# Values and output gates of the matrix memory as seven products of quarters, with row sums shared by GpSimd and VectorE

## The chip, the cores and the metric

One Trainium2 chip, of which the kernel uses one core. The metric is device time in microseconds: the median of the runs of the kernel on that core. Lower is better. The engines named are TensorE (PE; PEld are its weight loads), VectorE (DVE), ScalarE (ACT), GpSimd (POOL) and SyncE (SP), which issues the loads.

## What is computed

Two transformer-like blocks over 2048 tokens of width 1024, in float32. The first block norms and modulates its input, projects it with one wide matrix, and sends the parts to neighbourhood attention on a grid and to a matrix memory (mLSTM) that runs both ways over the sequence. The part that matters here, cut from the reference:

```python
proj = h @ w_in + b_in                      # h: 2048 x 1024
(..., ml_q, ml_k, ml_v, ml_o, ml_z, i_f, f_f, i_b, f_b) = jnp.split(proj, split_idx, axis=-1)
qk = jax.nn.silu(centred_short_conv(jnp.concatenate([ml_q, ml_k], axis=-1), conv_w, conv_b))  # 5 taps
h_fwd = mlstm_chunkwise(mq, mk, mv, i_f, f_f)
h_bwd = flip(mlstm_chunkwise(flip(mq), flip(mk), flip(mv), flip(i_b), flip(f_b)))
hm = (h_fwd + h_bwd) * jax.nn.sigmoid(ml_o)
hm = (hm - mu) * lax.rsqrt(var + EPS) * ml_norm_w
ml_out = hm * jax.nn.silu(ml_z)
```

There are 4 heads of 128 channels. `ml_v` (values) and `ml_o` (output gates) of a head are each the 2048 x 1024 rows times a 1024 x 128 slice of weights, plus a bias.

## The kernel before, in words

The function `mlstm` (L313) runs after `modulate_and_norm`, which leaves the normed rows turned in `hT` (128 partitions, 8 pieces of 128 channels, 2048 tokens). It is one block in which every engine has its own program, in program order, and the engines meet at semaphores. The order of the work is written out by hand. The heads are taken one after the other (head 0 to head 3 below; x in the code).

For each head there are three projections by channels (keys, queries, gate z): `project` (L578), 12 blocks of 8 matmuls 128x512 at L600 into `bank[0]` and `bank[1]`, evicted by ScalarE (`evict`, L745 and L750). Those of head x + 1 are spread over the state and chunk loops of head x, two matmuls at a time. Then, with nothing else on TensorE, comes the stage that the change rewrites: `project_turned` (L604 to L615), 8 blocks (4 of values, 4 of output gates), each 4 tiles of tokens x 8 matmuls 128x128 at L614, with tokens on the partitions of the result. VectorE adds the bias while it copies a block out (`put`, L854 to L866) into `v1` or `og`.

What the other engines do beside that stage: VectorE convolves the queries (`convolve`, L838: one tensor_scalar at L848 and four taps, scalar_tensor_tensor of 2048 columns, at L851) and scales the keys (`scale_keys`, L872), in the order of `values` (L925). For head 0 the five steps of the keys' convolution come first. ScalarE applies silu to the keys (L810) as soon as their convolution is done, then to the queries (L812) when theirs is, and only then enters the state loop.

The state loop has 15 steps: TensorE turns two chunks of keys (`turn`, L628), ScalarE weighs them (`weigh`, L757), TensorE multiplies them with the values (`product`, L637 to L645) and, behind that in its queue, runs two matmuls of the next head's projections; VectorE adds the result to the carried state (`carry`, L880). At its second step ScalarE applies the sigmoid to all of `og` (L819). In the chunk loop follow scores, decays, products with the state (L651, L656, L662) and sums (`add_up`, L903; `divide`, L917); GpSimd masks the rows of decays (`mask`, L542), adds both directions and multiplies by the gate (`combine`, L548 and L550). Then VectorE takes moments, norms (sixteen tensor_scalars, L1000), convolves the next head's keys, and scales the turned outputs into `mix` (`put_head`, L923), for which TensorE turns them (`turn_out`, L672) between projections. The order there is four times `turn_out`, two matmuls of projection, and then the next head's stage.

SyncE loads each weight slice (`load`, L451, issued at L459) when the product that used its room is done.

Of the kernel before, what the change touches and what calls it, by code (L numbers as in the profile page):

```python
# [8 lines left out]
ALU = mybir.AluOpType  # L9
# [3 lines left out]
P = 128  # L13
T = 2048
D = 1024
KC = D // P
# [296 lines left out]
def mlstm(nc, t, hT, mix, c_act, w_first, w_first_in, roll):  # L313
# [6 lines left out]
    with ExitStack() as ctx:  # L320
# [82 lines left out]
        out_dve = sem("l_out_dve")  # L403
# [30 lines left out]
        NB = 4 * NW  # L434
        NA = 4 * V_

# [7 lines left out]
        def evicted(n):  # L444

            return (out_act, n + 1, NA) if n < NA else (out_dve, n - NA + 1, NB - NA)

        with nc.Block() as block:
            @block.sync
            def _(sp):  # L450
                def load(x, s):  # L451
                    if x > LAST:
                        return
                    if s == O_ and x == LAST:
                        sp.wait_ge(proj, NB * x + 4)
                    elif x > 0:
                        sp.wait_ge(proj, NB * (x - 1) + 4 * s + 4)
# [10 lines left out]
                def fetch_bias(x):  # L468
                    if x > LAST:
                        return  # L470
                    need(sp, out_dve, (NB - NA) * x)
# [30 lines left out]
                for x in range(ML_HEADS):  # L502
# [16 lines left out]
                    if x == LAST - 1:  # L519
                        ada_v = t["w_ada"].rearrange("a (k p) n -> p (a k) n", p=P)  # L520
                        sp.wait_ge(proj, NB * ML_HEADS)
# [5 lines left out]
                sp.wait_ge(proj, NB * ML_HEADS)  # L527
# [9 lines left out]
            def _(pool):  # L537
                def mask(x, b):
                    pool.wait_ge(rb_in[b % 2], 16 * (2 * x + b // 2 + 1))
                    view = rb[:, b % 2].rearrange("p d (c l) -> p d c l", l=P)  # L540
                    for dr in range(2):
                        nc.gpsimd.tensor_tensor(view[:, dr], view[:, dr], causal[:, dr].unsqueeze(1).broadcast_to([P, 4, P]), ALU.add).then_inc(masked, 1)  # L542

# [22 lines left out]
                nc.gpsimd.memset(state[:, 0, 0], 0.0).then_inc(once, 1)  # L566
                nc.gpsimd.memset(state[:, NT - 1, 1], 0.0).then_inc(once, 1)
                pool.wait_ge(causal_in, 16)
                for x in range(ML_HEADS):
                    for b in range(NTB):  # L570
# [6 lines left out]
            def _(pe):  # L577
                def project(x, m0, m1):  # L578
# [3 lines left out]
                    for m in range(m0, m1):  # L582
                        n, k = divmod(m, KC)
                        s = n // 4
                        if k == 0:
# [9 lines left out]
                            elif x > 0:  # L595
                                done, value, each = evicted(NB + n - 2)
# [7 lines left out]
                def project_turned(x, n):  # L604
                    s = n // 4
                    if n % 4 == 0:
                        pe.wait_ge(w_in[s], 16 * (x + 1))
                    done, value, each = evicted(n - 2)
                    pe.wait_ge(done, each * x + value)
                    w = weights(x, s)  # L610
# [4 lines left out]
                    last.then_inc(proj, 1)  # L615

                def modulate(m0, m1):

                    for m in range(m0, m1):
                        n, k = divmod(m, KC)  # L620
                        if k == 0:
                            pe.wait_ge(ada_in[n], 16)
                            pe.wait_ge(out_dve, (NB - NA) * ML_HEADS)
# [3408 lines left out]
```

## Time and profile before

| | us |
|---|---|
| median of 3 runs | 3411.91 |
| lowest, highest | 3411.88, 3414.09 |
| the profiled execution | 3414.13 |
| its span, first to last instruction | 3412.3 |
| TensorE busy | 3307.3 |
| VectorE busy | 1310.2 |
| ScalarE busy | 1015.7 |
| GpSimd busy | 928.4 |

The trace holds one execution. Times in it are microseconds from the start of the span. A timeline row gives the start, the duration, the engine, the line, the operation with what it writes and reads, its shape and how many follow each other; in brackets stand the idle time before it and what ended that. A matmul in float32 has two records. Records of one engine can overlap by a few hundredths. A busy time is not a cost by itself: what counts is what TensorE waits for, and how long the engines' operations take beside each other.

### The profile page before, as it was taken

To read this page: it belongs to the slowest core of one execution; us is meant where nothing else is said; L and a number is where in the kernel's file an instruction comes from. 1 tells how busy PE (TensorE), PEld (TensorE's weight loads), DVE (VectorE), ACT (ScalarE), POOL (GpSimd) and SP (SyncE) were. 2 spreads that over 40 slices of the span, in tenths; PEclk is the share of its full clock that TensorE was granted. 3 is DMA by queue.
4 is the path that set the end of the run, shared out by engine and by line. 5 is a ranking of instruction groups with operands and counts; after the bars stand their busy time and mean duration, and the time that the engine had idled before them with its cause. 6 is when DMAs were issued, how large, how long until landed. Compare 5 with 4: busy or idle time off the path is not lost. (4 is left out here: it accounts for less than half of the span.)

```text
span 3412.3 us, 43811 instructions
## 1 busy us (share of the span) xinstructions
PE 3307.3 (97%) x16379; PEld 1809.4 (53%) x16379; DVE 1310.2 (38%) x2804; ACT 1015.7 (30%) x2409; POOL 928.4 (27%) x705
## 2 busy tenths in 40 slices
PE   8999999998999999898999999999999999999999
PEld 4485858584455455444454545454545454545544
DVE  3334444446244244444333323332433243545522
ACT  4314141413324144233233423342334143411100
POOL 1002020205442532633311152115211521161232
PEclk9999999999999999999999999999999999999999
DMA  6101010113021112332061646254634464340321
GB/s 226 35 25 38 21 38 13 33 41 96 25 48 20 49 31 83 122 108 79 22 35 32 40 100 51 32 45 106 43 29 49 108 40 26 59 117 13 142 93 62
DMA packets 282365, 202.43 MB, mean 59 GB/s; under 512 B 124380, under 2 KB 249708, under 8 KB 278528
## 3 DMA queue, kind: packets, MB, share of 16 engines
q1 hardware_dynamic: 279052, 199.62, 30.8%
q8 instruction: 132, 2.16, 0.3%
q14 instruction: 77, 0.63, 0.1%
q10 hardware_dynamic: 3104, 0.01, 0.1%
HBM read 153.79 MB, written 45.81 MB: 58 GB/s over the span
## 5 line engine op out<-in xcount | busy, mean ns | idle before, releaser
L2465 PE MATMUL d<-hT,roll 128*128 128x512 f32 x1280 | 579.4, 596 | 2.1 <-PEq L76 2.1
L2465 PE MATMUL d<-w_room,roll 128*128 128x512 f32 x960 | 435.6, 596 | 2.3 <-DVE w_room L2429 2.3
L2465 PEld LDWEIGHTS d<-hT,roll 128*128 128x128 f32 x1280 | 242.4, 191 | 300.8 <-issue 299.3
L600 PE MATMUL m<-hT,roll 128*128 128x512 f32 x704 | 321.1, 593 | 1.3 <-ACT pre L750 1.3
L2465 PEld LDWEIGHTS d<-w_room,roll 128*128 128x128 f32 x960 | 181.1, 190 | 224.6 <-issue 222.8
L2502 POOL TENSOR_TENSOR w_z<-w_u,w_y 128x512 f32<-128x512 f32 x40 | 50.7, 1267 | 796.4 <-ACT w_y L2471 787.3
L1412 PE MATMUL n<-hT,roll 128*128 128x512 f32 x512 | 227.6, 600 | 1.8 <-PEq L76 1.8
L600 PEld LDWEIGHTS m<-hT,roll 128*128 128x128 f32 x704 | 124.9, 191 | 116.0 <-issue 115.8
L1412 PE MATMUL n<-mix_na,roll 128*128 128x512 f32 x384 | 169.4, 594 | 0.5 <-POOL roll L1312 0.5
L548 POOL TENSOR_TENSOR hn<-hn 128x512 f32<-128x512 f32 x16 | 17.5, 1093 | 543.3 <-DVE hn L917 543.3
L1412 PEld LDWEIGHTS n<-hT,roll 128*128 128x128 f32 x512 | 97.1, 192 | 123.3 <-issue 122.9
L3125 ACT ACTIVATE mix_f<-sneg,negmax 128x192 f32<-128x192 f32 (+1 forms) x384 | 160.6, 423 | 5.6 <-DVE negmax L3239 3.6
L614 PEld LDWEIGHTS m<-roll,hT 128*128 128x128 f32 x1280 | 143.6, 192 | 2.4 <-issue 1.4
L614 PE MATMUL m<-roll,hT 128*128 128x128 f32 x1280 | 143.9, 275 | 0.7 <-DVE v L866 0.7
L1412 PEld LDWEIGHTS n<-mix_na,roll 128*128 128x128 f32 x384 | 71.7, 190 | 87.3 <-issue 85.1
L3239 DVE CUSTOM_DVE_ANT_0 sneg<-d,bias 128x192 f32<-128x192 f32 (+1 forms) x384 | 108.8, 323 | 23.8 <-PE d L2970 14.6
L3671 PE MATMUL f<-hT,roll 128*128 128x512 f32 x256 | 113.5, 600 | 2.6 <-DVE mix_f L3868 1.4
L2494 DVE TENSOR_TENSOR w_u<-d,w_u 128x512 f32<-128x512 f32 x64 | 44.3, 691 | 166.1 <-PE d L2465 110.9
L2936 PE MATMUL d<-sq,ones 128*128 128x512 f32 x192 | 98.8, 596 | 4.1 <-ACT sq L3091 4.1
L3096 ACT ACTIVATE rt<-d,eps 128x512 f32<-128x512 f32 x96 | 66.0, 687 | 108.4 <-PE d L2936 108.4
L2984 PE MATMUL d<-ident,mix_f 128*128 128x128 f32 x600 | 86.1, 280 | 10.6 <-ACT mix_f L3125 9.1
L3002 PE MATMUL d<-roll,mix_f 128*64 128x64 f32 x2400 | 91.0, 226 | 0.6 <-DVE mix_f L3266 0.6
(403 smaller groups left out, 5205.8 us busy)
## 6 DMA issues: line engine op xcount, KB each, us to landing
roll<-in_w_in SPq DMA_DIRECT2D x128, 256.0 KB, 3.1
mix_f<-alpha SPq DMA_DIRECT2D x48, 192.0 KB, 6.1
xg<-in_x SPq DMA_DIRECT2D x4, 2048.0 KB, 16.2
roll<-in_w_in SPq DMA_DIRECT2D x16, 512.0 KB, 3.8
rb<-r_rows SPq DMA_DIRECT2D x16, 512.0 KB, 4.8
mix_ml<-in_x SPq DMA_DIRECT2D x16, 512.0 KB, 3.3
x<-mix_ml SPq DMA_DIRECT2D x16, 512.0 KB, 3.0
o_rows<-mix_f SPq DMA_DIRECT2D x8, 1024.0 KB
```

What stands on the lines that cost most here:

```text
L600: last = nc.tensor.matmul(bank[n % 2][:], w[:, k], hT[:, k, (n % 4) * TB:(n % 4 + 1) * TB], start=(k == 0), stop=(k == KC - 1))
L614: last = nc.tensor.matmul(bank[n % 2][:, j * P:(j + 1) * P], hT[:, k, c * P:(c + 1) * P], w[:, k], start=(k == 0), stop=(k == KC - 1))
L1412: last = nc.tensor.matmul(bank_of(f, i)[:], w[:, k], xs[k], start=(k == 0), stop=(k == h - 1))
L2465: last = nc.tensor.matmul(bank[self.bank_of(n, j, i)][:], w[:, k], x[k], start=(k == 0), stop=(k == h - 1))
L2502: nc.gpsimd.tensor_tensor(self.z[:], u, self.y[:], ALU.add).then_inc(self.pooled, 1)
L2936: nc.tensor.matmul(bank[S_BANK][:], ones[:], sq[:, e % 2], start=True, stop=True).then_inc(ssq, 1)
L2984: last = nc.tensor.transpose(bank[T_BANK + j][:, i * P:(i + 1) * P], prob[:, u % (2 * BU), part_ * P:(part_ + 1) * P], ident[:])
L3002: last = nc.tensor.matmul(bank[O_BANK][h * half:(h + 1) * half, (u % BU) * half:(u % BU + 1) * half], vals[:, v, h * half:(h + 1) * half], ...
L3096: nc.scalar.activation(rt[:, e % 2], bank[S_BANK][:], ACT.Ln, bias=epst[:, 0:1], scale=1.0 / half).then_inc(rooted, 1)
L3125: nc.scalar.activation(prob[:, u % (2 * BU), off:off + n], sneg[:, (U * a + u) % 6, 0:n], ACT.Exp, bias=negmax[:, c, u:u + 1], scale=-1.0, ...
L3239: nc.vector.tensor_tensor_reduce(out=sneg[:, (U * a + u) % 6, 0:n], in0=bank[b][:, c0:c0 + n], in1=bias[:, i % 2, c, t0:t0 + n], scale=1.0 ...
L3671: last = nc.tensor.matmul(bank_of(f, i)[:], w[:, k], xs[k], start=(k == 0), stop=(k == h - 1))
```

## The change

The products are taken two tiles of tokens at a time (a pair p, 8 of them) and with the 1024 channels in two halves. With the two token tiles as rows and the two halves as columns of a 2x2 matrix of quarters, and the weights' halves of values and output gates as another, seven products of quarters with sums take the place of eight. Each product (`vo_product`) is 4 matmuls 128x128 and has a bank of its own; even and odd pairs use the two halves of the 256 columns. The order of products within a pair is 1, 4, 2, 3, 6, 5, 7. Products 2, 4, 5 and 6 read sums of rows (`vo_sum`: four operations 128x512 per pair, made by GpSimd for even pairs and by VectorE for odd ones, in the room of `state`); 2, 4, 5 and 7 read sums of weights (`vo_weights`: four operations 128x512 per head on GpSimd, one of them in place, the others in the rooms of `dm`, `kw` and `sd`). VectorE adds up what the banks hold after each odd pair (`read`: seven operations of 256 columns), and GpSimd makes two sums of 256 columns between them (`vo_join`, one before product 6 is read, one after product 5).

What moves with it: the last tap of the queries' convolution stands behind the last `read`; `scale_keys` stands ahead of the first; GpSimd's first masks of a head and two memsets of `state` stand behind its share of the stage; the loads of the next head's value and gate weights wait for all products of the stage; TensorE's stage begins only when ScalarE has evicted all 12 blocks of projections.

```diff
-        NB = 4 * NW
         NA = 4 * V_
+        HK = KC // 2
+        NP = NT // 2
+        VO = (1, 4, 2, 3, 6, 5, 7)
+        vo_sums = state[:, :, :, :].rearrange("p c d l -> p (c d l)")[:, 0:2 * 4 * HK * P].rearrange("p (s m k n) -> p s m k n", s=2, m=4, n=P)
+        T2, T3, T4 = (x[:, :, :, :].rearrange("p a b l -> p (a b) l") for x in (dm, kw, sd))
...
         def evicted(n):
 
-            return (out_act, n + 1, NA) if n < NA else (out_dve, n - NA + 1, NB - NA)
+            return (out_act, n + 1, NA) if n < NA else (vo_read, 7 * NTB, 7 * NTB)
...
+        def vo_sum(eng, engine, x, p):
+
+            done = vo_s[p % 2]
+            n0 = 16 * x + 4 * (p // 2)
+            if p >= 2:
+                eng.wait_ge(vo_prod, 7 * NP * x + 7 * (p - 1))
+            elif x == 0:
+                eng.wait_ge(gturned, GB)
+            else:
+                eng.wait_ge(crossed, NT * x)
+                eng.wait_ge(carried, 2 * NS * x)
...
+            engine.tensor_tensor(s1, a21, a22, ALU.add).then_inc(done, 1)
+            eng.wait_ge(done, n0 + 1)
+            engine.tensor_tensor(s2, s1, a11, ALU.subtract).then_inc(done, 1)
+            engine.tensor_tensor(s3, a11, a21, ALU.subtract).then_inc(done, 1)
+            eng.wait_ge(done, n0 + 2)
+            engine.tensor_tensor(s4, a12, s2, ALU.subtract).then_inc(done, 1)
...
                     if s == O_ and x == LAST:
-                        sp.wait_ge(proj, NB * x + 4)
+                        sp.wait_ge(proj, NA * x + 4)
+                    elif s >= V_:
+                        need(sp, vo_prod, 7 * NP * x)
...
+                def values(x):
+                    for i in (3, 1, 2):
+                        vo_weights(x, i)
+                    vo_sum(pool, nc.gpsimd, x, 0)
+                    vo_weights(x, 4)
+                    vo_sum(pool, nc.gpsimd, x, 2)
+                    vo_join(x, 0)
+                    vo_sum(pool, nc.gpsimd, x, 4)
+                    vo_join(x, 1)
+                    vo_sum(pool, nc.gpsimd, x, 6)
+                    vo_join(x, 2)
+                    vo_join(x, 3)
+                    pool.wait_ge(vo_prod, 7 * NP * (x + 1))
+                    nc.gpsimd.memset(state[:, 0, 0], 0.0).then_inc(state_zero, 1)
+                    nc.gpsimd.memset(state[:, NT - 1, 1], 0.0).then_inc(state_zero, 1)
...
                 for x in range(ML_HEADS):
+                    values(x)
                     for b in range(NTB):
                         mask(x, b)
...
-                def project_turned(x, n):
...
-                    for j in range(4):
-                        c = 4 * (n % 4) + j
-                        for k in range(KC):
-                            last = nc.tensor.matmul(bank[n % 2][:, j * P:(j + 1) * P], hT[:, k, c * P:(c + 1) * P], w[:, k], start=(k == 0), stop=(k == KC - 1))
...
+                def vo_product(x, p, i):
...
+                    lhs, rhs = {1: (rows(0, c0), wv[:, 0:HK]), 2: (sum_of(1), T2), 3: (rows(HK, c0), wv[:, HK:KC]), 4: (sum_of(0), wo[:, 0:HK]),
+                                5: (sum_of(2), T3), 6: (sum_of(3), wo[:, HK:KC]), 7: (rows(HK, c1), T4)}[i]
+                    if p == 0 and i in (2, 4, 5, 7):
+                        pe.wait_ge(vo_made, 4 * x + {5: 1, 4: 2, 2: 3, 7: 4}[i])
+                    if i in (2, 4, 5, 6):
+                        pe.wait_ge(vo_s[p % 2], 16 * x + 4 * q + {4: 1, 2: 2, 5: 3, 6: 4}[i])
+                    if q >= 1 and p % 2 == 0:
+                        pe.wait_ge(vo_read, 7 * (NTB * x + q - 1) + VO.index(i) + 1)
+                    for k in range(HK):
+                        last = nc.tensor.matmul(vo_bank(i)[:, p % 2 * P:(p % 2 + 1) * P], lhs[k], rhs[:, k], start=(k == 0), stop=(k == HK - 1))
+                    last.then_inc(vo_prod, 1)
+
+                def values(x):
+                    pe.wait_ge(out_act, NA * (x + 1))
...
+                        pe.wait_ge(h_out, NTB * x)
...
+                    for p in range(NP):
+                        for i in VO:
+                            vo_product(x, p, i)
...
                 def turn(x, i):
                     if i >= 2:
                         pe.wait_ge(k_weighed, 2 * (NS * x + i - 1))
-                    elif x > 0:
-                        pe.wait_ge(h_out, NTB * x)
+                    elif i == 0:
+                        pe.wait_ge(vo_read, 7 * (NTB * x + NTB - 1) + VO.index(3) + 1)
...
                     if i == 0:
-                        pe.wait_ge(out_dve, (NB - NA) * x + 4)
+                        pe.wait_ge(vo_read, 7 * NTB * (x + 1))
...
                         if i == 1:
-                            act.wait_ge(out_dve, (NB - NA) * (x + 1))
+                            act.wait_ge(vo_read, 7 * NTB * (x + 1))
+                            act.wait_ge(vo_pooled, 2 * NTB * (x + 1))
                             nc.scalar.activation(og[:], og[:], ACT.Sigmoid).then_inc(o_ready, 1)
...
+                def read(x, q):
...
+                    for m, i in enumerate(VO):
+                        dve.wait_ge(vo_prod, 7 * (NP * x + 2 * q + 1) + m + 1)
+                        if i in (3, 2):
+                            dve.wait_ge(vo_read, r0 + 1)
+                        elif i in (6, 5):
+                            dve.wait_ge(vo_pooled, 2 * (NTB * x + q) + 1)
...
+                        nc.vector.tensor_tensor(dst, src, other, ALU.add).then_inc(vo_read, 1)
...
+                    nc.vector.tensor_tensor(bias_more, vo_b[:, 1], vo_b[:, 0], ALU.subtract).then_inc(bias_out, 1)
+                    vo_sum(dve, nc.vector, x, 1)
                     convolve(x, Q_, 0)
-                    put(x, NA)
-                    convolve(x, Q_, 1)
-                    convolve(x, Q_, 2)
-                    put(x, NA + 1)
-                    convolve(x, Q_, 3)
+                    scale_keys(x)
+                    dve.wait_ge(bias_out, x + 1)
+                    for q in range(NTB - 1):
+                        read(x, q)
+                        vo_sum(dve, nc.vector, x, 2 * q + 3)
+                        convolve(x, Q_, q + 1)
+                    read(x, 3)
                     convolve(x, Q_, 4)
-                    for n in range(NA + 2, NB):
-                        put(x, n)
-                        if n == NA + 3:
-                            scale_keys(x)
```

## Rows read from the trace of the kernel before

**Rows 1.** The page, busy time and share of the span, all engines

```profile
PE 3307.3 (97%) x16379; PEld 1809.4 (53%) x16379; DVE 1310.2 (38%) x2804; ACT 1015.7 (30%) x2409; POOL 928.4 (27%) x705
```

**Rows 2.** Groups by line, L614; columns: busy us, mean ns, idle before

```profile
L614 PE MATMUL m<-roll,hT 128*128 128x128 f32 x1280 | 143.9, 275 | 0.7 <-DVE v L866 0.7
...
L614 PE MATMUL m<-mix_ml,hT 128*128 128x128 f32 x768 | 86.2, 275 | 0.0
```

**Rows 3.** Timeline, head 1, its stage's start and end: start us, us, engine

```profile
358.82 28.75 PE L614 MATMUL m<-roll,hT 128*128 128x128 f32 x256
...
416.00 0.60 PE L634 MATMUL m<-ident,roll 128*128 128x128 f32 x4
...
416.41 1.14 ACT L757 ACTIVATE kw<-m,gates 128x128 f32<-128x128 f32 x4 [35.73 <-PE m L634]
...
417.09 0.71 PE L645 MATMUL m<-v,kw 128*128 128x129 f32 x4 [0.50 <-ACT kw L757]
```

**Rows 4.** Groups by line and form, and L851 by itself (min/median/max ns)

```profile
L2502 POOL TENSOR_TENSOR w_z<-w_u,w_y 128x512 f32<-128x512 f32 x40 | 50.7, 1267 | 796.4 <-ACT w_y L2471 787.3 <-DMA v_rows<-w_z 9.1
...
L3412 DVE TENSOR_TENSOR w_room<-w_room 128x511 f32<-128x511 f32 x4 | 2.8, 692 | 0.1
...
L887 DVE TENSOR_TENSOR sd<-m,dm 128x256 f32<-128x256 f32 x64 | 26.7, 422 | 50.1 <-PE m L651 47.2 <-issue 2.5 <-ACT dm L765 0.2
...
L851 DVE SCALAR_TENSOR_TENSOR roll<-pre,small,roll x32: 2340/2352/3243, 189.4 to 717.2; 128x2048 f32<-128x2048 f32 x32
```

**Rows 5.** Timeline, GpSimd and VectorE in head 0

```profile
187.76 1.56 DVE L848 TENSOR_SCALAR roll<-pre,small 128x2048 f32<-128x2048 f32 x1
...
188.19 2.25 POOL L542 TENSOR_TENSOR rb<-rb,causal 128x512 f32<-128x512 f32 x1
...
189.36 3.24 DVE L851 SCALAR_TENSOR_TENSOR roll<-pre,small,roll 128x2048 f32<-128x2048 f32 x1
...
190.40 3.32 POOL L542 TENSOR_TENSOR rb<-rb,causal 128x512 f32<-128x512 f32 x1
```

**Rows 6.** Timeline, GpSimd and VectorE in the dilated attention stage

```profile
1639.38 4.53 POOL L2433 TENSOR_TENSOR hT<-hT 128x2048 f32<-128x2048 f32 x1
...
1640.83 0.69 DVE L2494 TENSOR_TENSOR w_z<-d,w_z 128x512 f32<-128x512 f32 x1 [2.74 <-PE d L2465]
```

**Rows 7.** Timeline, head 0, the stage's start and end

```profile
185.36 0.21 POOL L566 MEMSET state<- 128x129 f32 x1 [22.03 <-PE m L695]
...
187.05 0.69 ACT L745 ACTIVATE mix_ml<-m,small 128x512 f32<-128x512 f32 x1 [7.94 <-PE m L600]
...
187.24 14.51 PE L614 MATMUL m<-roll,hT 128*128 128x128 f32 x128
...
245.48 0.60 PE L634 MATMUL m<-ident,roll 128*128 128x128 f32 x4
```

**Rows 8.** Timeline, head 1, the silu of the queries

```profile
378.69 2.00 ACT L812 ACTIVATE roll<-roll,small 128x2048 f32<-128x2048 f32 x1 [17.09 <-DVE roll L851]
```

**Rows 9.** Timeline, from head 0's last chunk to head 1's stage

```profile
329.68 1.18 POOL L550 TENSOR_TENSOR og<-og,hn 128x512 f32<-128x512 f32 x1
...
338.74 4.19 DVE L1000 TENSOR_SCALAR og<-og,mv,rs 128x128 f32<-128x128 f32 x16
...
354.49 0.63 PE L672 MATMUL m<-ident,og 128*128 128x128 f32 x4 [0.36 <-DVE mix_ml L923]
...
359.02 0.69 ACT L745 ACTIVATE mix_ml<-m,small 128x512 f32<-128x512 f32 x1 [8.49 <-PE m L600]
```

**Rows 10.** Windows: busy us and records of PE, PEld, DVE, ACT, POOL; granted clock; DMA

```profile
759.60:762.20 2.60, 0.01 (x1) 0.00 (x0) 0.49 (x2) 2.59 (x5) 0.00 (x0) 1.00 1.04 406
...
1420.90:1424.20 3.30, 0.00 (x0) 0.00 (x0) 0.54 (x2) 2.63 (x5) 3.30 (x3) 0.86 0.63 202
...
59.25:64.40 5.15, 5.15 (x24) 5.15 (x25) 2.92 (x5) 4.35 (x8) 0.00 (x0) 0.50 0.00 0
...
1424.20:1430.00 5.80, 5.79 (x13) 3.45 (x14) 2.81 (x5) 3.95 (x8) 0.65 (x1) 0.50 0.68 224
```

More of the change, by code:

```diff
@@ L470, in fetch_bias @@
                         return
-                    need(sp, out_dve, (NB - NA) * x)
+                    need(sp, vo_read, 7 * NTB * x)
                     h = heads[x]
@@ new lines, in vo_join @@
+                def vo_join(x, q):
+                    _, y, u, z = (temps[:, q % 2, m] for m in range(4))
+                    r0 = 7 * (NTB * x + q)
+                    pool.wait_ge(vo_read, r0 + 3)
+                    if q == 0:
+                        need(pool, gated, NTB * x)
+                        need(pool, h_turned, NTB * x)
+                    nc.gpsimd.tensor_tensor(z, u, y, ALU.add).then_inc(vo_pooled, 1)
+                    pool.wait_ge(vo_read, r0 + 6)
+                    nc.gpsimd.tensor_tensor(vo_chunks(og, q, 1), u, y, ALU.add).then_inc(vo_pooled, 1)
@@ L595, in project @@
                             elif x > 0:
-                                done, value, each = evicted(NB + n - 2)
+                                done, value, each = evicted(NA)
                                 pe.wait_ge(done, each * (x - 1) + value)
@@ L602, in project @@
                                 last.then_inc(proj, 1)
-                def project_turned(x, n):
[L605 to L610, printed above, removed]
-                    for j in range(4):
-                        c = 4 * (n % 4) + j
-                        for k in range(KC):
-                            last = nc.tensor.matmul(bank[n % 2][:, j * P:(j + 1) * P], hT[:, k, c * P:(c + 1) * P], w[:, k], start=(k == 0), stop=(k == KC - 1))
-                    last.then_inc(proj, 1)
+                def vo_product(x, p, i):
+                    c0, c1, q = 2 * p, 2 * p + 1, p // 2
+                    wv, wo = weights(x, V_), weights(x, O_)
+                    rows = lambda k0, c: [hT[:, k0 + k, c * P:(c + 1) * P] for k in range(HK)]
+                    sum_of = lambda m: [vo_sums[:, p % 2, m, k] for k in range(HK)]
+                    lhs, rhs = {1: (rows(0, c0), wv[:, 0:HK]), 2: (sum_of(1), T2), 3: (rows(HK, c0), wv[:, HK:KC]), 4: (sum_of(0), wo[:, 0:HK]),
[9 more added lines that the diff above has]
+                    last.then_inc(vo_prod, 1)
@@ L701, in _ @@
                     nc.tensor.matmul(bank[2 + dr][:, 0:NT * ML_HEADS], pick[:, dr], gates[:, :, dr, 1, :], start=True, stop=True).then_inc(picked, 1)
-                pe.wait_ge(once, 6)
+                pe.wait_ge(once, 4)
                 for x in range(ML_HEADS):
-                    for n in range(NA, NB):
-                        project_turned(x, n)
+                    values(x)
                     pe.wait_ge(k_ready, x + 1)
```

91 lines of the change are left out of this document (71 added, 20 removed).

## The prediction

> **What bounds the kernel now.** The page's busy shares come first: TensorE is busy 97% of the span [rows 1], so matmuls saved in a stretch without gaps are time saved, and any new gap on TensorE is time lost. The groups by line then price the work that the change replaces: 1280 + 768 records at L614, the projection of values and output gates [rows 2]. They are 1024 float32 matmuls of 128 columns, two records each. The timeline of head 1 shows the stage without a gap: its first matmul starts at 358.82 us and the turning of the keys at 416.00 [rows 3]. So 57.18 us for 512 records, 0.1117 us each. What is to be seen around the stage is that ScalarE, VectorE and GpSimd have slack in it; the question is whether the change keeps TensorE fed.
>
> **What is saved.** Per head 256 matmuls become 8 pairs x 7 products x 4 = 224, so 57.18 us become 50.03: 7.15 us a head, 28.6 us in all. Work moves to where it is added and copied: four sums a pair, four sums of weights a head, 28 instead of 8 copies out of the banks.
> The Trainium skill, "TensorE: Matmul & The Clock Gate", section "Back-to-back issue gap", gives about 81 ns for one of a sustained stream of 128-column matmuls with their weight loads; by that the 256 records saved would be worth 20.7 us and the total would be 3441.7 us, still inside the range of (A). The trace prices this very stream at 0.1117 us, and that is used.
>
> **The price that decides the rest: sums on two engines.** Alone, a 128x512 operation of GpSimd on two SBUF tensors takes 1.27 us, one of half the columns at least 0.64 (I take 0.7); VectorE's of 512 columns 0.69, a convolution tap 2.35, an operation out of a bank with 256 columns 0.42 [rows 4]. Beside each other they do not overlap [rows 5]: GpSimd's mask of 188.19 lasts until 190.44, 1.12 us behind the end of VectorE's tensor_scalar at 189.32; the tap issued at 189.36 ends at 192.60, 2.16 us behind 190.44; the next mask, issued at 190.40, ends at 193.72, 1.12 us behind 192.60. So one instruction runs, the other engine's waits for its end, and they take turns: a GpSimd op then costs 1.12, a tap 2.16. A VectorE addition that reads a bank is free of it: 0.69 us in the middle of a GpSimd op of 4.53 [rows 6].
>
> **Head 0, start.** GpSimd comes to the new work at about 185.4 (its state memset there ran at 185.36), ScalarE's last eviction ends at 187.74, TensorE's stage ran from 187.24 to 245.48 [rows 7]. TensorE now waits for that eviction: start at 187.8, 0.55 late. GpSimd gets two weight sums done by 188.0. There VectorE begins the five taps of the keys (187.76 in the trace), and turns begin: 1.08 + 1.12 for the first tap and the third weight sum, then four times 2.16 + 1.12 for taps and the four sums of pair 0: the last sum ends at 188.0 + 2.2 + 13.1 = 203.3, the fourth weight sum at 204.5. Product 6 needs that last sum: TensorE does product 1, waits 4.8 us for the first sum (193.5), 2.4 for the second, and 4.8 for the last; products 6, 5, 7 end pair 0 at 206.05, where 194.05 would be unhindered: 12.0 us lost. VectorE, which still has its sums for pair 1, a tap and the key scaling in front of the first copies, is ready at 212.9, pair 1 ends at 212.3: 0.65 lost.
>
> **The middle.** Two pairs of products take 12.5 us. VectorE: seven copies 2.9, sums 2.65, tap 2.35. GpSimd: sums 5.1, joins 1.4. In order: GpSimd sums during the odd pair while VectorE copies from banks (no turns); the join comes after the sums, at 6.2 us, so copies 5 to 7 end at 7.5; VectorE's sums and tap follow with one turn lost (0.4) and end at 12.8; the next copy is due at 13.6, the sums at 13.4 and were ready at 10.4. Covered, with 0.8 us to spare on VectorE; if that cover goes, each of the three rounds loses what is over. I take 0.
>
> **The end of the stage, each head.** The fifth tap of the queries now stands behind the last copy, and ScalarE's queue is: silu of keys, silu of queries, then the first weighing of keys. Before, that silu ran at 378.69, 37 us ahead of need [rows 8], and TensorE's first state product came 1.09 us behind the turning, at 417.09 [rows 3]. After: release 0.2, copy 0.42, tap 2.35, silu 2.00, two weighings 0.66 (four took 1.14), release 0.08: 5.7 us. TensorE's queue holds that product in front of the next head's projections, so 4.6 us are lost in each of four heads: 18.5. Behind VectorE's tap stands only the first carry, needed after the third product. GpSimd's two state memsets (0.2 us each) now come after the last product and end before that carry; the masks behind them serve exponentials some 40 us later. SyncE's loads of the next value and gate weights wait for the whole stage instead of half of it: issued near 252 us, needed at 330.9, so free. The key scaling, moved ahead of the first copies, finds its silu 2.9 us into the stage and ends 3 us before the first copy: free too, and so are the bias subtraction and pair 1's sums there.
>
> **Heads 1 to 3, start.** TensorE waits for ScalarE's eviction of 359.02, 0.69 long: 0.95 us. GpSimd starts its eight operations at 330.9, behind the gating of the head before, and is busy until 341.2; VectorE's sixteen tensor_scalars start at 338.74 [rows 9], so two turns of 1.12 fall among them: 2.2 us (1.1 if GpSimd is a tenth faster). That lands on a path with no slack: TensorE already waits 0.36 for VectorE's put_head at 354.49, and VectorE goes there from the tensor_scalars without a pause. TensorE's turning of the outputs waits 2.2 us longer.
>
> **The clock.** In a gap of 3.3 us the granted clock fell (mean 0.86), and then stood at 0.50, 1.2 of 2.4 GHz, for 5.8 us of matmuls; another low stretch lasted 5.15 us; a gap of 2.6 left it at 1.00 [rows 10]. The new gaps of about 5 us are longer than the first. Half speed for 5.2 to 5.8 us loses 2.7. Head 0 loses it there too, and again at 203.4 (2.7, less 0.65 that then no longer waits for VectorE: 2.1). Heads 1 and 2: 2.7 each. Head 3 has no projections to slow: 0.3.
>
> **Sum.** Head 0: 0.55 + 12.0 + 0.65 + 2.1 - 7.15 - 1.06 (its stage took 58.24, head 1's 57.18: waits that go) = 7.1 inside, + 4.6 + 2.7 = 14.4. Heads 1 and 2: 0.95 + 2.2 - 7.15 + 4.6 + 2.7 = 3.3 each. Head 3: the same with 0.3 for the clock, 0.9. Together +21.9. The profiled execution took 3414.13 us around its span of 3412.3, 2.2 above the median 3411.91 of the runs shown; the stages after are the same, so the shift goes to the median: 3433.8.
>
> **Bounds.** Without any loss to the clock +11.4; with GpSimd a tenth faster besides, +8. The other way: 0.1 us more in each of VectorE's twelve steps and the join eats the slack and adds 0.5 in each of twelve rounds, 6; the low clock as long as 7 us adds 3; a second gap in head 0 that slows more products, 3: +34.
>
> **Rivals.**
> (A) The forecast: order of the queues and turns, TensorE starved at the stage's two ends. For: every wait is in the code, every price in a row. Against: durations are taken for shapes not yet run. 3420 to 3446, chance 0.76.
> (B) VectorE bounds the middle too: reads, sums and tap need more than 12.5 us, by 1 us or more a round. Against: the margin worked out; for: it is only 0.8. 12 x 1 to 2 us on top: 3446 to 3460. Chance 0.12.
> (C) No change: the two engines run side by side for these shapes, and short gaps leave the clock. Then in head 0 the last sum of pair 0 ends at 194.4 instead of 203.3, pair 1 waits for VectorE's first sum at 199.3 (five taps, then the sum), together 4.4 lost, and the stage gains 3.3: +1.3 with the end wait. Heads 1 to 3: 0.95 - 7.15 + 4.6 = -1.6 each. Total -3.5, 3408.4. Against: every pair of neighbours in [rows 5], and the gap of 3.3 us in [rows 10]. Chance 0.08.
> (D) Faster, the other side: the silu of queries does not stand in the way, as if the first weighing came before it. That takes back 4.6 us a head and its clock loss; with (C)'s side-by-side sums it gives 3408.4 - 18.5 = 3390. It decides where a head's gain of 7.15 exceeds its waits by 1.7 (6.8 over four heads). Against: ScalarE's rows stand in program order everywhere. Chance 0.04.
>
> **Numbers.** About 0.2% (6.8 us) is what a measurement here can tell from none. Slower by more: A and B, 0.88; within: C, 0.08; faster: D, 0.04. The range takes A's bounds with a little of each side: 3418 to 3447.
>
> **What would show it.** In the changed trace: 1792 records of products, 0.11 us each; in head 0 the sums of pair 0 alternating with taps until about 203, products 6 at 203.4; silu of queries behind the last tap, and a gap of about 5 us in front of the first state product in each head, with clock 0.50 behind it in heads 0 to 2; tensor_scalars of the normalisation spread over 6.4 us instead of 4.2; no gap between pairs 2 and 7. It would be wrong if GpSimd's sums overlap taps at full speed, if gaps appear inside the middle, or if the clock stays at 1.00 behind the end gap (then +11).

## The result, and the profile after

The changed kernel takes **3434.1 us** (median of 4 runs, 3431.0 to 3436.7) against 3413.0 (3411.9 to 3415.6) for the kernel before on the same chip: ratio 1.006, 95% interval 1.0043 to 1.0078, slower by 21 us. The forecast was 3433.8. The profiled execution of the changed kernel is the fastest of the four, 3431.0 us with a span of 3429.2, so sums over the trace are made against that: 16.9 us over the span of before.

The page of the changed kernel, busy time and share of the span, to be held against [rows 1]:

```profile
PE 3292.0 (96%) x16123; PEld 1790.0 (52%) x16123; DVE 1387.3 (40%) x2952; ACT 1015.5 (30%) x2409; POOL 1069.3 (31%) x823
```

TensorE has 256 records less and is busy 15.3 us less, not 28.6: more of what is left runs at half clock (windows below). VectorE has 77 us more work, GpSimd 141.

TensorE's timeline at the end of the stages of heads 0 and 1, beside [rows 3, 7] (start us, us, engine, line, out<-in, in brackets the wait before and its releaser):

```profile
251.91 0.60 PE L747 MATMUL m<-ident,roll 128*128 128x128 f32 x4
...
257.39 1.23 PE L758 MATMUL m<-v,kw 128*128 128x129 f32 x4 [4.88 <-ACT kw L869]
...
424.52 0.60 PE L747 MATMUL m<-ident,roll 128*128 128x128 f32 x4
...
430.00 1.23 PE L758 MATMUL m<-v,kw 128*128 128x129 f32 x4 [4.88 <-ACT kw L869]
...
431.03 3.62 PE L695 MATMUL m<-hT,roll 128*128 128x512 f32 x4
```

The stage of head 1 starts at 374.39 (row below), so it takes 50.13 us where it took 57.18: the products save what they should. The first state product comes 5.48 us behind the turning of the keys, before 1.09. The four projection matmuls behind it then take 3.62 us, and 1.88 at full clock. All engines there:

```profile
425.06 2.34 DVE L964 SCALAR_TENSOR_TENSOR roll<-pre,small,roll 128x2048 f32<-128x2048 f32 x1
...
427.44 2.00 ACT L924 ACTIVATE roll<-roll,small 128x2048 f32<-128x2048 f32 x1 [51.21 <-DVE roll L964]
429.35 1.12 ACT L869 ACTIVATE kw<-m,gates 128x128 f32<-128x128 f32 x4
```

The last copy starts at 424.72; read down from there: last tap, silu of the queries, weighing of the keys, each behind the one above. ScalarE had been idle for 51 us, waiting for that tap.

The start of head 0's stage on GpSimd, VectorE and TensorE:

```profile
190.63 3.30 POOL L482 TENSOR_TENSOR state<-hT 128x512 f32<-128x512 f32 x1
...
200.44 3.31 POOL L487 TENSOR_TENSOR state<-hT,state 128x512 f32<-128x512 f32 x1
```
```profile
189.58 13.05 DVE L964 SCALAR_TENSOR_TENSOR roll<-pre,small,roll 128x2048 f32<-128x2048 f32 x4
```
```profile
188.35 1.13 PE L713 MATMUL m<-roll,hT 128*128 128x128 f32 x8 [0.47 <-ACT mix_ml L857]
194.08 2.05 PE L713 MATMUL m<-mix_ml,state 128*128 128x128 f32 x8 [4.60 <-POOL state L482]
197.35 2.04 PE L713 MATMUL m<-dm,state 128*128 128x128 f32 x8 [1.22 <-POOL state L484]
...
203.81 2.08 PE L713 MATMUL m<-mix_ml,state 128*128 128x128 f32 x8 [3.06 <-POOL state L487]
```

Sums of 3.3 us against 1.27 alone, taps of 3.26 against 2.34: they take turns, TensorE waits three times, and head 0's stage takes 63.56 us (188.35 to 251.91) instead of 58.24.

From head 0's last chunk to head 1's stage, beside [rows 9]:

```profile
351.39 1.26 POOL L487 TENSOR_TENSOR state<-hT,state 128x512 f32<-128x512 f32 x1
351.61 5.95 DVE L1128 TENSOR_SCALAR og<-og,mv,rs 128x128 f32<-128x128 f32 x16
352.61 1.27 POOL L611 TENSOR_TENSOR sd<-roll,dm 128x512 f32<-128x512 f32 x1
...
369.11 0.63 PE L785 MATMUL m<-ident,og 128*128 128x128 f32 x4 [2.12 <-DVE mix_ml L1048]
```
```profile
374.39 1.16 PE L713 MATMUL m<-roll,hT 128*128 128x128 f32 x8 [0.78 <-ACT mix_ml L857]
...
714.46 0.63 PE L785 MATMUL m<-ident,og 128*128 128x128 f32 x4 [2.13 <-DVE mix_ml L1048]
```

The sixteen scalings take 5.95 us for 4.19, and TensorE's wait for the head's copies is 2.12 for 0.36: the same 1.76. The last row is the same wait ahead of head 3's stage.

Windows, with the granted clock as the third column from the end: the wait of head 1, what follows it, the same behind head 0, and a stretch ahead of head 3:

```profile
425.10:430.00 4.90, 0.02 (x1) 0.00 (x0) 2.30 (x2) 2.56 (x4) 4.90 (x5) 0.89 0.90 233
430.00:435.60 5.60, 5.60 (x14) 3.42 (x15) 0.61 (x2) 4.15 (x6) 2.19 (x2) 0.50 0.04 10
...
257.40:261.60 4.20, 4.20 (x8) 2.26 (x9) 0.61 (x2) 3.65 (x4) 2.19 (x2) 0.50 0.04 10
715.20:719.00 3.80, 3.80 (x9) 1.95 (x8) 0.98 (x2) 0.00 (x0) 0.00 (x0) 0.56 0.00 0
```

**Where the time went.** The first state products of heads 0 to 3 are late against before by 10.75, 12.91, 15.77 and 19.02 us. Head 0: 1.11 at the start, 5.32 in the stage, 4.32 at its end. Head 1 adds 2.16, and the rows give 2.1 (half of the stretch at 257.4) + 1.76 + 0.78 - 7.05 + 4.39 = 1.98. Head 2 adds 2.86; the rows give 2.8 behind 430.0 and the same -0.12, 2.68. Head 3 adds 3.25; the rows give -0.12 and two low stretches, one behind head 2's wait at the stage's end and one at 715.2, of 1.7 us each, 3.3. Of the 19.02 some 2 are given back in later stages, in which no instruction is changed. The two largest falls stand where the clock differs: the lag falls by 1.2 us where before has the low clock for 7.0 us (1423.2 to 1430.2) and the changed kernel for 3.6 (1442.6 to 1446.2), and by 1.7 where before has it for 3.6 us (2966.0 to 2969.6) and the changed kernel not at all. Why the clock differs there is open.

### The profile page after: what moved, and what is told of

Same layout as the page of the kernel before. It is cut to its first block and busy times, and to the rows that moved or that the text cites. A ratio compares the mean times of both kernels' runs of the same rounds, so it can differ in the third digit from the quotient of the medians.

```text
span 3429.2 us, 43754 instructions
## 1 busy us (share of the span) xinstructions
PE 3292.0 (96%) x16123; PEld 1790.0 (52%) x16123; DVE 1387.3 (40%) x2952; ACT 1015.5 (30%) x2409; POOL 1069.3 (31%) x823
## 5 line engine op out<-in xcount | busy, mean ns | idle before, releaser
L1833 DVE TENSOR_TENSOR vo<-n,vo 128x512 f32<-128x512 f32 x48 | 33.2, 691 | 148.9 <-PE n L1540 144.1
L3130 PEld LDWEIGHTS d<-roll,mix_f 128*64 128x64 f32 x2400 | 78.0, 137 | 23.7 <-issue 23.7
```

The costliest lines, as they stand in the source:

```text
L3130: last = nc.tensor.matmul(bank[O_BANK][h * half:(h + 1) * half, (u % BU) * half:(u % BU + 1) * half], vals[:, v, h * half:(h + 1) * half], ...
```

## The experiments

Runs 1 to 7 each change one thing in the changed kernel (3434.1 us, stage starts and waits as above); run 8 puts four of them together, run 9 builds on it. The kernel before, timed beside them, took 3411.6 us (runs 1 to 4), 3412.7 (5 to 8) and 3413.3 (9).

**1. The last query tap ahead of the last copies.**

```diff
                         convolve(x, Q_, q + 1)
-                    read(x, 3)
                     convolve(x, Q_, 4)
+                    read(x, 3)
```

> The last query tap stands in VectorE's queue ahead of the fourth quarter's seven reads instead of behind them; nothing else changes. Theory (the order of VectorE's and ScalarE's queues makes the wait at the end of the stage): the tap ends some 4 us before the turn, ScalarE's silu of the queries runs while TensorE still multiplies, and the first state product follows the turn by 1.1 us as in the kernel before, not by 5.5 us. That is 4.4 us for each of 4 heads, 17.6, and most of the clock loss behind the gap in heads 0 to 2 (2.7 each): 3434 - 17.6 - 6 to 8, so 3408 to 3411 us. Rival 1 (VectorE has no room in the last quarter: the tap of 2.34 us pushes the reads back by as much as it saves): the gap falls by 2 us at most, 3424 to 3428 us. Rival 2 (the gap belongs to the seven products' own reads and joins): no change, 3431 to 3437 us.

Measured: 3409.0 us (3406.2 to 3410.7), against 3411.6 for before in the same session, ratio 0.9992 (0.9982 to 1.0001). Timeline of head 1:

```profile
412.24 0.42 DVE L989 TENSOR_TENSOR hn<-m,vo_b 128x256 f32<-128x256 f32 x1
412.36 2.00 ACT L924 ACTIVATE roll<-roll,small 128x2048 f32<-128x2048 f32 x1 [44.36 <-DVE roll L964]
...
416.30 0.60 PE L747 MATMUL m<-ident,roll 128*128 128x128 f32 x4
...
417.39 0.71 PE L758 MATMUL m<-v,kw 128*128 128x129 f32 x4 [0.50 <-ACT kw L869]
```

The silu is over before the keys are turned, and the product comes 1.09 us behind. VectorE's first copy of the last quarter starts 1.0 us later than in the changed kernel, the fourth is on time again: rival 1 falls. From head 0's first state product to head 1's and on to head 2's it is now 166.11 us each (before 170.46), so heads 1 and 2 gain 4.35 each. Head 3 takes 167.81 and gains 2.66, since the clock is low at 694.0 to 697.6 us, behind the wait for head 2's copies. Head 0's product is 4.64 late, which takes back part of the 11.4. One moved line is worth 22 us between the profiled spans (3429.2 and 3406.8) and 25 between the medians, and turns the change from a loss into no measurable difference.

**2. The silu moved instead of the tap.**

```diff
-                    act.wait_ge(conv, n_conv * (2 * x + 2))
-                    nc.scalar.activation(qT[:], qT[:], ACT.Silu, bias=small[:, h, 15:16]).then_inc(soft_q, 1)
                     for i in range(NS):
                         weigh(x, i)
                         if i == 1:
+                            act.wait_ge(conv, n_conv * (2 * x + 2))
+                            nc.scalar.activation(qT[:], qT[:], ACT.Silu, bias=small[:, h, 15:16]).then_inc(soft_q, 1)
```

> The tap stays behind the last read; ScalarE's silu of the queries, with its wait for that tap, is moved from ahead of the first weighing of the keys to behind the second. Theory (the first product waits for ScalarE's in-order queue, not for the tap itself): the gap between turn and first state product goes to about 1.1 us although the tap still ends at the same time; some of it can come back at the third product, since silu and sigmoid now stand together in front of the third weighing (2.3 for the tap, 2.0 silu, 1.3 table, 1.9 sigmoid: weighing at about +8 us after the turn, while two products and four projections give TensorE 7.6 us of work at full clock): 3434 - 17.6 - 6, plus 0 to 4, so 3410 to 3416 us. Rival (VectorE's tap bounds it, since it stands in front of the carries): the gap or the wait for the carries keeps 2 us or more each head, 3420 to 3428 us. No change, 3431 to 3437, if neither queue is the cause.

Measured: 3424.6 us (3422.5 to 3426.1), in the rival's range and outside the theory's. Timeline of head 1:

```profile
422.34 0.60 PE L747 MATMUL m<-ident,roll 128*128 128x128 f32 x4
...
422.88 2.34 DVE L964 SCALAR_TENSOR_TENSOR roll<-pre,small,roll 128x2048 f32<-128x2048 f32 x1
...
423.44 0.71 PE L758 MATMUL m<-v,kw 128*128 128x129 f32 x4 [0.50 <-ACT kw L869]
...
425.26 2.00 ACT L929 ACTIVATE roll<-roll,small 128x2048 f32<-128x2048 f32 x1 [1.36 <-DVE roll L964]
...
428.58 1.91 ACT L932 ACTIVATE og<-og 128x2048 f32<-128x2048 f32 x1
430.39 1.12 ACT L869 ACTIVATE kw<-m,gates 128x128 f32<-128x128 f32 x4
431.05 1.23 PE L758 MATMUL m<-v,kw 128*128 128x129 f32 x4 [2.58 <-ACT kw L869]
432.07 2.85 PE L695 MATMUL m<-hT,roll 128*128 128x512 f32 x4
```

The first product comes 1.10 us behind the turn while the tap is still running: not the tap but ScalarE's queue held it, and nobody waits for the first carry, at 425.14 behind the tap. But the third product now waits 2.58 us for the third weighing, behind silu, table load (1.28) and sigmoid, and the clock falls again. The expectation gave TensorE 7.6 us of cover; its work ends 6.1 us behind the turn (428.47), where the third product has to wait. The rival's mechanism (the tap in front of the carries) isn't in the trace; its number came out by another one.

**3. Work in the gap.** Nineteen matmuls of 128x128 into a bank that nobody reads, between the second turn and the first product; they give nothing to the output.

```diff
+                        if i == 0:
+                            pe.wait_ge(vo_read, 7 * NTB * (x + 1))
+                            for j in range(19):
+                                nc.tensor.matmul(bank[7][:, 0:P], kT[:, 0:P], ident[:], start=True, stop=True)
                         product(x, i)
```

> Between the second turn and the first state product TensorE does 19 matmuls of 128x128 into a bank that nobody reads, some 4.3 us, which fills its wait at the end of the stage; the waits themselves stay, so the fill alone gives nothing. Theory (the wait also costs clock: the projections behind it run at 1.2 GHz in heads 0 to 2): the turn-to-product time stays 5.5 us, the granted clock stays 1.0 behind it, and each of heads 0 to 2 gives back about 2.7 us: 3424 to 3428 us. Rival (the clock falls for another reason, or comes back as a phase elsewhere): 3431 to 3437 us. If the fill is longer than the wait, it adds its surplus times 4.

Measured: 3423.5 us (3421.9 to 3426.4). Timeline of head 1:

```profile
424.24 0.60 PE L747 MATMUL m<-ident,roll 128*128 128x128 f32 x4
424.92 4.51 PE L827 MATMUL m<-ident,roll 128*128 128x128 f32 x38
429.72 0.71 PE L758 MATMUL m<-v,kw 128*128 128x129 f32 x4 [0.30 <-ACT kw L873]
430.27 1.88 PE L695 MATMUL m<-hT,roll 128*128 128x512 f32 x4
```

The time is 0.5 us below the theory's range. The product still comes 5.48 us behind the turn, and the projections behind it take 1.88 us instead of 3.62. The profiled spans differ by 6.5 us; the medians by 10.6, of which part is the spread of the two kernels. One stretch came back elsewhere: the clock stood at 0.50 behind the 2.1 us wait for head 0's copies (368 to 371 us), where it had stayed at 1.00 in the changed kernel. The rival named such a stretch elsewhere, but the time is far from its range. So the waits cost about 17.6 us themselves (four times 4.39), and 6 to 10 more through the clock. The Trainium skill describes the same on its page "TensorE: Matmul & The Clock Gate", "HAM oscillation — how this bites in real kernels": a wait of TensorE is paid again as slow matmuls behind it.

**4. The key taps of head 0 narrowed.**

```diff
+                        w = 64 if x == 0 and s == K_ else T
-                        last = nc.vector.scalar_tensor_tensor(out=dst[:], in0=pre[:, s, j:j + T], scalar=wj, in1=dst[:], op0=ALU.mult, op1=ALU.add)
+                        last = nc.vector.scalar_tensor_tensor(out=dst[:, 0:w], in0=pre[:, s, j:j + w], scalar=wj, in1=dst[:, 0:w], op0=ALU.mult, op1=ALU.add)
```

> Left out: in head 0 the second to fifth tap of the key convolution are computed for 64 of the 2048 columns only (the first stays whole); their waits and order stay. Theory (the GpSimd sums of the first pair of chunks took turns with the key taps on the port to SBUF): GpSimd's four sums take 1.3 us each instead of 3.3 until VectorE's own sums start, the last of them ends at 196 to 197.5 us instead of 203.8, TensorE's three waits in head 0 (4.6, 1.2, 3.1 us) shrink to 2 us or less together, and the clock doesn't fall: head 0's stage from 63.6 to 53 to 56 us, the time 3423 to 3427 us. Rival (GpSimd is simply slow on these shapes in head 0, or waits for the seven products' weights): sums still 3 us or more each, the stage over 60 us, and the time falls by under 4 us.

The output of this run is incomplete, since most of the taps' columns are left out. Measured: 3424.0 us (3421.9 to 3426.7), in the theory's range. Timeline of head 0:

```profile
187.72 4.96 DVE L965 SCALAR_TENSOR_TENSOR roll<-pre,small,roll 128x64 f32<-128x64 f32 x4
188.76 1.26 POOL L482 TENSOR_TENSOR state<-hT 128x512 f32<-128x512 f32 x1
...
190.16 2.04 PE L713 MATMUL m<-mix_ml,state 128*128 128x128 f32 x8 [2.54 <-POOL state L482]
...
192.55 1.27 POOL L487 TENSOR_TENSOR state<-hT,state 128x512 f32<-128x512 f32 x1
```

GpSimd's sums take 1.27 us again and end at 193.8, even before the range given; two of the three waits are gone, the third is 2.54 us (2 or less was expected), and the stage takes 55.50 us instead of 63.56. The clock, which was to stay, still fell: it is low from 188.8 to 195.8 us, from inside the wait that is left. The row on VectorE is the clearest picture of the turns: a tap of 64 columns lasts 1.24 us on average, the time of the GpSimd operation that it waits for.

**5. GpSimd's last two early operations behind the key taps, heads 1 to 3.**

```diff
             eng.wait_ge(done, n0 + 2)
+            if p == 0 and x > 0:
+                eng.wait_ge(conv, n_conv * (2 * x + 1))
             engine.tensor_tensor(s4, a12, s2, ALU.subtract).then_inc(done, 1)
```

> In heads 1 to 3 the last of GpSimd's eight operations ahead of the stage but one (the fourth sum of the first pair), and so the last weight difference behind it, wait until the key taps are done; they then run beside the head's copies from matrix memory and not beside the 16 scalings of the norm. Theory (those scalings stretched from 4.19 to 5.95 us because the two engines take turns): they take 4.2 us again, TensorE's wait for the copies falls from 2.1 to 0.4 us in each of three heads, and the clock drop behind the last of these waits (3.9 us at half clock, 2 us lost) goes: 3434 - 5.3 - 2, so 3425 to 3429 us. Rival 1 (the scalings are slow for another reason): 3431 to 3437 us. Rival 2 (the two delayed operations now take turns with the key taps or hold up the stage's first products): slower than 3437 us.

Measured: 3425.5 us (3422.5 to 3428.2), in the theory's range. Timeline ahead of head 1's stage:

```profile
349.93 4.19 DVE L1130 TENSOR_SCALAR og<-og,mv,rs 128x128 f32<-128x128 f32 x16
...
365.01 1.27 POOL L489 TENSOR_TENSOR state<-hT,state 128x512 f32<-128x512 f32 x1 [15.26 <-DVE roll L966]
365.67 0.63 PE L787 MATMUL m<-ident,og 128*128 128x128 f32 x4 [0.36 <-DVE mix_ml L1050]
```

Scalings 4.19 us, TensorE's wait 0.36, no low clock ahead of head 3. Both rivals fall; the two operations lie beside copies that read a bank.

**6. Head 0 by the scheme of before.** `project_turned` and `put` come back for x == 0, with their queues, and the counts of the semaphores start one head later:

```diff
                 def values(x):
+                    if x == 0:
+                        for n in range(NA, NA + 8):
+                            project_turned(x, n)
+                        return
...
```

> Head 0 is projected by the sixteen-by-sixteen scheme of the kernel before, with its queues; heads 1 to 3 keep the seven products. Theory (head 0 has 61.7 us of two-input work on VectorE and GpSimd, which take turns, for a stage of 50 us, so that seven products can't pay there): head 0's stage takes 58.2 us again, its first state product comes 1.1 us behind the turn, and the clock behind it stays: the product at 246.7 to 247.3 us instead of 257.4, the second head's stage starts 12 to 13 us earlier, 3420 to 3423 us. Rival (the loss of head 0 is a one-time cost of entering the scheme, such as the first weight differences, and moves to head 1): head 1's stage is longer than 51 us and the time 3428 us or more.

Measured: 3420.4 us (3415.1 to 3424.8), in the theory's range. Timeline of head 0:

```profile
188.20 14.51 PE L731 MATMUL m<-roll,hT 128*128 128x128 f32 x128
...
246.44 0.60 PE L769 MATMUL m<-ident,roll 128*128 128x128 f32 x4
247.59 0.71 PE L780 MATMUL m<-v,kw 128*128 128x129 f32 x4 [0.56 <-ACT kw L891]
```

58.24 us again, head 1's stage starts at 362.48 instead of 374.39 and still takes 50.13. So the loss is head 0's own and doesn't move on. That the sum of work (61.7 us in the expectation) is its cause isn't shown by this: in the changed kernel all of head 0's waits stand in its first pair, and from 203.81 us to the turn at 251.91 TensorE has none.

**7. The wait at the stage's start split**: product 1 waits for eleven evictions, the twelfth stands before the first product of the other bank.

```diff
+                    if p == 0 and i == 2:
+                        pe.wait_ge(out_act, NA * (x + 1))
+                    if p == 0 and i == 3 and x > 0:
+                        pe.wait_ge(h_out, NTB * x)
...
-                    pe.wait_ge(out_act, NA * (x + 1))
+                    pe.wait_ge(out_act, NA * x + 11)
...
-                        pe.wait_ge(h_out, NTB * x)
```

> The first product waits for eleven of the head's twelve evictions, the second product on the other bank for the twelfth; the wait for the head's copies moves to the product that writes their bank. Theory: TensorE's wait of 0.8 us ahead of each stage (heads 1 to 3; 0.55 in head 0) shrinks to 0.1 or nothing: 3434 - 2 to 3, so 3430 to 3433 us. In head 0 the wait for the first sum takes what is won, so the stage there doesn't end earlier. Rival (the wait moves to the next product, which needs a sum or the other bank as late): 3433 to 3436 us.

Measured: 3431.8 us (3428.4 to 3434.0), in the theory's range, but its runs overlap the changed kernel's, so the time alone doesn't show it. The trace does: in heads 1 to 3 the stage starts without a wait and takes 50.03 us; in head 0 the 0.47 us wait is still there.

**8. Edits 1, 5, 6 and 7 together.**

> Four edits together: the last query tap ahead of the last reads (measured alone 3409.0 us), head 0 by the scheme of the kernel before, GpSimd's last two operations ahead of heads 1 to 3 behind the key taps, and the split of the wait at the stage's start. Theory: heads 1 to 3 each take 50.1 instead of 57.2 us with nothing given back: 3412 - 3 x 7.05 = 3391 us, plus 0 to 3 for what is left of the old waits: 3390 to 3395 us, faster than both kernels. Rival (the waits reappear at other places or as clock drops, as the silu's did): 3397 us or more.

Measured: **3391.0 us** (3388.4 to 3393.6, 5 runs) against 3412.7 (3408.6 to 3415.4): ratio 0.9938 (0.9925 to 0.9950). It beats both kernels. TensorE at the start of head 1's stage and at its end, then at head 3's third product, and the same product in the kernel before:

```profile
358.79 1.05 PE L724 MATMUL m<-roll,hT 128*128 128x128 f32 x8
```
```profile
408.81 0.60 PE L774 MATMUL m<-ident,roll 128*128 128x128 f32 x4
409.91 0.71 PE L785 MATMUL m<-v,kw 128*128 128x129 f32 x4 [0.50 <-ACT kw L896]
...
740.78 1.23 PE L785 MATMUL m<-v,kw 128*128 128x129 f32 x4 [2.66 <-ACT kw L896]
```
```profile
762.27 0.71 PE L645 MATMUL m<-v,kw 128*128 128x129 f32 x4 [2.65 <-ACT kw L757]
```

From one head's first state product to the next it is 163.3 us each time, before 170.46: 7.15 us a head, and three times that is 21.5 of the 21.7 measured. The rival's clock drop is there once, in a small size: the wait of 2.66 us at head 3's third product is the one of 2.65 that before has too, but here the product behind it runs at half clock (low from 740.6 to 744.2 us) and the lead over before shrinks from 21.5 to 20.2 us. Later stages bring the lead of the profiled spans to 23.2.

**9. The same with all row sums on VectorE.** GpSimd keeps the differences of the weights and the joins.

```diff
-                    vo_sum(pool, nc.gpsimd, x, 0)
...
+                    vo_sum(dve, nc.vector, x, 0)
                     vo_sum(dve, nc.vector, x, 1)
...
+                        vo_sum(dve, nc.vector, x, 2 * q + 2)
                         read(x, q)
```

> The kernel of the four edits (3391.0 us) with the row sums of heads 1 to 3 all on VectorE; GpSimd keeps the weight differences and the joins. Theory (in heads 1 to 3 VectorE has room for both halves: in a quarter of 12.5 us it would do 2.9 us of reads, 2 x 3.0 of sums and 2.3 of a tap, 11.2 together, and its sums take 0.69 us each against GpSimd's 1.26): no change, 3388 to 3395 us. Rival (the second half of the sums makes VectorE late, so that TensorE waits for a sum or a read in each quarter): TensorE's gaps in the stage grow by 1 us or more a head, 3395 to 3405 us.

Measured: 3389.8 us (3387.8 to 3390.2), ratio 0.9929 (0.9913 to 0.9946), not to be told from 3391.0. VectorE and TensorE:

```profile
379.76 0.42 DVE L1013 TENSOR_TENSOR hn<-m,vo_b 128x256 f32<-128x256 f32 x1
```
```profile
408.29 0.60 PE L771 MATMUL m<-ident,roll 128*128 128x128 f32 x4
```

The copies of this quarter start 21.50 us into the stage behind the added sums, and 19.85 us into it in run 8 (378.64 less 358.79). TensorE, which started this stage at 358.26, still has no gap in it (50.03 us). In heads 1 to 3 the sharing of the sums by the two engines earns nothing.

## Why the prediction was right, and where its terms were off

The case was (A), and its mechanism holds in its main steps: the products save what was worked out, and what is lost lies at the stage's two ends. Against the time of before shown with the prediction the shift is 22.2 us, forecast 21.9; against before on the same chip it is 21.1, and over the profiled spans 16.9.

- **What is saved**, 7.15 us a head at 0.1117 a record: heads 1 to 3 take 50.13, 7.05 less, and 50.03 once the start's wait is gone. Held. By the 81 ns of the Trainium skill ("TensorE: Matmul & The Clock Gate", "Back-to-back issue gap"), taken for a record as in the prediction, it would be about 5.2, an estimate; here the trace decides.
- **Head 0's turns**, 12.0 + 0.65 + 2.1: the last sum of pair 0 ended at 203.75 against 203.3. The waits were 8.9 (4.6, 1.2, 3.1) for 12.0, but the clock fell at 194 already and not only at 203, so that slow products filled part of the wait; the clock cost about 4 for 2.1. The 0.65 for VectorE's lateness didn't come: its copies started at 210.85 (212.9 worked out), since three of its four sums took 0.68 to 0.69 us, with no operation of GpSimd beside them. Stage 5.3 us longer plus its late start, 6.4 for the 7.1 forecast, 0.5 of it a shift that ScalarE's eviction ahead has too. So 8.9 and 4 stand for 12.0 and 2.1: the sum came out because one error covers the other. Run 4 shows the turns as the cause, run 6 that this loss is head 0's alone.
- **The end wait**, 4.6 a head: 4.39 (5.48 for 5.7 worked out). Held, and runs 1 and 2 show the queue of ScalarE as its cause. That one moved tap takes this wait away was not seen: the prediction took the order as fixed.
- **Turns with the scalings**, 2.2: 1.76, and it landed on TensorE whole, as said; run 5 shows it.
- **The start's wait**, 0.95: 0.78 in the bracket.
- **The clock behind the end wait**, 2.7 in heads 0 to 2: 2.1, 2.8, 1.7, mean 2.2. The low stretches begin inside the wait (254.8 for a wait that ends at 257.39, 428.8 for 430.0), so part of each costs nothing. The prediction read its second low stretch short: the 5.15 us from 59.25 are the matmuls of a stretch of 7.0 us, from 57.8 to 64.8, that begins in a gap. Head 3, 0.3: nothing; its slow products lie ahead of a wait for a weighing that before has too.
- **Not foreseen**: a drop of 1.7 behind the wait for head 2's copies, for which the sum has no term. The added 1.76 us brings it about: each of the seven kernels with a wait of 2.1 us there (the changed one and runs 1 to 4, 6 and 7) has one such drop, in one of three heads, and before and runs 5, 8 and 9 have none.
- **The middle at nothing**: no gap in it, and run 9 shows that VectorE had far more room than the 0.8 us counted: its copies start 1.7 us later there and TensorE has no gap. A pair's four sums on VectorE, put at 2.65 us, took 2.84 (413.06 to 415.90), the first of them 0.91; it didn't matter.
- (C) falls by the rows of head 0 and by run 4: the two engines took turns.

Adding the measured sizes gives 10.75, 2.16, 2.86 and 3.25, together 19.0 at head 3's product, for 21.6 forecast there. The agreement of the medians to 0.3 us is luck within their spread of 5.7; the steps together are off by 2.6 us at head 3's product, and by 5 over the profiled spans.

## What to carry to other kernels

Where an added step is cheap, ask which in-order queue it closes: one tap behind the last copies held a silu, the silu held a weighing, the weighing held TensorE, 4.4 us in each head for 2.3 us of work that fits a few instructions earlier. When work is split over VectorE and GpSimd, look at what the other engine has in its queue at the time when TensorE needs the first results: four key taps there made GpSimd's first four sums take 3.3 us for 1.27. By my estimate from the rows, such work in head 0 comes to some 61 us (twenty sums of GpSimd at 1.27 us and eight joins at 0.73, sixteen sums of VectorE at 0.69 and eight taps at 2.34) for a stage of 50, but the waits stood in the first pair alone, which points at the order at the start and not at the sum. Try the version with one engine as well: here it was as good. And where the same stage is run several times, look whether one of them has other neighbours: from the stage's start to the first state product, head 0 took 59.4 us in run 8 by the old scheme and 64.8 in run 1 by the new one. Whether another order would make the new scheme pay in head 0 as well was not run.

## What the runs showed of the hardware

- Turns are paid by the short side too: taps of 64 columns beside GpSimd sums of 1.27 us lasted 1.24 us each (run 4), a bias subtraction of 128 columns 1.35 us in head 0 and 0.28 in the others. GpSimd's memsets are free of it; one of 0.20 us, at 425.14, ran inside the tap of 425.06. The Trainium skill says so on its page "SBUF — State Buffer", "Who interferes with whom": two SBUF inputs on VectorE contend with a GpSimd operation that reads SBUF, not with one that only writes. The same section of the Trainium skill says that tensor_scalar, with one input, can contend too. The scalings agree: 5.95 us for 4.19, and 4.19 again in run 5.
- A wait of the same length may cost the clock or not. In the changed kernel a wait of 2.12 us for a head's copies left it at 1.00 ahead of head 1 (368 to 371 us), and one of 2.13 us was followed by 0.56 ahead of head 3 (715.2 to 719.0); in run 3 it was the first of these places that fell. The wait of 2.65 us at head 3's third product left it at 1.00 in the kernel before, and one of 2.66 at the same place was followed by the low clock in run 8. The 4.9 us waits cost it each time in the changed kernel, and the matmuls behind them ran slow for 3.3 to 5.8 us in heads 0 to 2.
- The stage's start in head 0 differed by 2.1 us between profiled executions of kernels that are the same up to there (186.37 in run 2, 188.47 in run 3), so starts of single traces are not compared to less than that. It goes with the first low stretch of the clock, near 40 us: where that lasts 3.6 us (runs 1, 2, 4 and 5) the stage starts at 186.4 to 186.5, where it lasts 7.0 (before, runs 8 and 9) at 186.7 to 187.2, and where it lasts 10.4 (the changed kernel, runs 3, 6 and 7) at 188.2 to 188.7. Distances from product to product within one kernel repeat to 0.01 where the clock doesn't fall.
